# Memory value products placed inside the causal attention of a two-block transformer kernel

## The reference, cut to what matters

```python
mem_n = rms_norm(mem, mem_norm_w)
y_rnn = recurrent_group(...)
y_att = chunk_band_attention(q, k, v, rel_bias)      # 8 heads of 64, causal by chunks of 64
mixed = concatenate([rms_norm(y_rnn, gn_rnn_w), rms_norm(y_att, gn_att_w)])
x = x + mixed @ w_out
h = rms_norm(x, ln2_w)
k = mem_n @ wk                                       # memory keys
v = mem_n @ wv                                       # memory values: 256 x 1024
x = x + memory_cross_attention(h, ...)
```

## Time and profile before

| what | us |
|---|---|
| median of 3 runs | 2440.44 (2439.38 to 2442.5) |
| the profiled execution, its own time | 2438.64 |
| its span, first to last instruction | 2436.5 |
| PE, DVE, ACT, POOL busy in the span | 2192.2, 1583.9, 1187.4, 207.2 |
| memory value products on PE | 191.6 to 217.1 |
| causal attention, first shift on DVE to last values on PE | 221.3 to 286.9 |

### The profile page before, as it was taken

The page is one execution under the profiler, slowest core; times in us unless marked ns, Lnnn a source line. Parts: engine busy times, 40 slices in busy tenths (PEclk is TensorE's granted clock), DMA queues, the critical chain, the costliest instruction groups (busy, mean ns, idle before and its releaser), DMA issues.

```text
span 2436.5 us, 27159 instructions
## 1 busy us (share of the span) xinstructions
PE 2192.2 (90%) x10362; PEld 1740.6 (71%) x10362; DVE 1583.9 (65%) x1884; ACT 1187.4 (49%) x1437; POOL 207.2 (9%) x155
## 2 busy tenths in 40 slices
PE   6987798959999999994897989999989888999997
PEld 4785577648788788783764768888766566888885
DVE  6435643338888888886578576465658857655565
ACT  4534534237777777775456442222245564222223
POOL 1000000020011010110001002011100100210120
PEclk9998899979999999997899999999999999999998
DMA  5232031357999999994310022222322001222321
GB/s 196 87 139 104 1 121 52 138 157 261 359 360 353 357 363 360 351 350 183 122 52 35 25 80 103 88 91 102 110 79 87 35 1 70 104 96 90 108 87 52
DMA packets 48814, 359.98 MB, mean 148 GB/s; under 512 B 12224, under 2 KB 13416, under 8 KB 21456
## 3 DMA queue, kind: packets, MB, share of 16 engines
q1 hardware_dynamic: 36880, 340.89, 37.9%
q0 software_dynamic: 10752, 13.60, 1.8%
q10 hardware_dynamic: 1088, 4.19, 0.4%
HBM read 360.71 MB, written 25.72 MB: 159 GB/s over the span
## 4 chain that ended last, share of the span: by engine, by line
PE 75%; DVE 10%; ACT 9%; issue 3%; DMA 2%; POOL 0%; ACTq 0%; SPq 0%; DVEq 0%; POOLq 0%
PE bank L1029 39%; PE bank L496 15%; PE bank L1940 10%; DVE split_products L560 3%; ACT split_products L724 2%; PE bank L1965 2%; PE bank L1742 1%; PE bank L486 1%; PE bank L1756 1%; ACT S L1806 1%; PE bank L1727 1%; DVE split_weights L1235 1%; DVE X L1280 1%; ACT S L759 1%; DMA S<-rows_scratch,idx 1%
## 5 line engine op out<-in xcount | busy, mean ns | idle before, releaser
L1029 PE MATMUL bank<-split_x_high,split_weights 128*128 128x512 f32 x2144 | 670.9, 393 | 31.2 <-DVE split_x_low L1249 14.7
L1243 ACT ACTIVATE split_weights<-ring 128x2048 fp32r<-128x2048 f32 (+1 forms) x122 | 228.2, 1872 | 657.7 <-PE bank L1029 523.7
L1029 PEld LDWEIGHTS bank<-split_x_high,split_weights 128*128 128x128 f32 x2144 | 406.6, 190 | 121.4 <-issue 36.8
L1235 DVE TENSOR_TENSOR split_weights<-ring,split_weights 128x2048 fp32r<-128x2048 f32 (+1 forms) x122 | 276.6, 2268 | 224.7 <-ACT split_weights L1243 224.6
L1029 PE MATMUL bank<-split_products,split_weights 128*128 128x512 f32 x1200 | 333.2, 394 | 4.5 <-DVE split_products L1435 4.5
L1029 PE MATMUL bank<-split_x_low,split_weights 128*128 128x512 f32 x800 | 312.9, 391 | 0.0
L1029 PEld LDWEIGHTS bank<-split_products,split_weights 128*128 128x128 f32 x1200 | 228.6, 191 | 53.8 <-DVE split_products L1435 6.0
L496 PE MATMUL bank<-split_products 128*128 128x512 f32 x768 | 188.9, 395 | 11.9 <-DVE split_products L560 11.9
L496 PE MATMUL bank<-split_x_high,split_products 128*128 128x512 f32 x768 | 190.0, 397 | 8.0 <-DVE split_x_high L560 8.0
L496 PE MATMUL bank<-split_x_low,split_products 128*128 128x512 f32 x768 | 189.9, 397 | 6.5 <-DVE split_x_low L560 4.4
L560 DVE TENSOR_TENSOR split_products<-ring,split_products 128x2048 fp32r<-128x2048 f32 x63 | 144.4, 2293 | 57.4 <-ACT split_products L724 57.3
(11 more groups left out here) (421 smaller groups left out, 2978.5 us busy)
## 6 DMA issues: line engine op xcount, KB each, us to landing
ring<-in_expert_down_w SPq DMA_DIRECT2D x32, 2048.0 KB, 9.1
ring<-in_expert_gate_w SPq DMA_DIRECT2D x31, 2048.0 KB, 8.8
ring<-in_expert_up_w SPq DMA_DIRECT2D x31, 2048.0 KB, 8.1
ring<-in_ffn_w_up SPq DMA_DIRECT2D x44, 1024.0 KB, 4.8
ring<-in_w_in SPq DMA_DIRECT2D x26, 1024.0 KB, 4.8
ring<-in_ffn_w_down SPq DMA_DIRECT2D x16, 1024.0 KB, 4.8
ring<-in_w_out SPq DMA_DIRECT2D x12, 1024.0 KB, 4.8
ring<-in_ffn_w_down SPq DMA_DIRECT2D x8, 768.0 KB, 4.1
```

The costliest lines, as they stand in the source:

```text
L1029: mm = pe.matmul(acc[:, :], w[:, u, k, m], x, start=first and q == 0, stop=last and q == 2)
L1235: st.tell(dve.tensor_tensor(w[:, 1, 0:ks, 0:nc_], raw_half(g)[:, :, 0:nc_], as_f32(w[:, 0, 0:ks, 0:nc_]), ALU.subtract), wl_done)
L1243: st.tell(act.activation(WHL[g % 2][:, 0, 0:ks, 0:nc_], raw_half(g)[:, :, 0:nc_], ACT.Copy), wh_done)
```

## The change

The memory value products leave their place ahead of the attention and are made inside it: PE's `pe_pairs` gets a function `fill`, called in each step between the values of `p - 2` and the transposes of `p - 1`. In each odd step `memory_values(p)` makes one of the eight tiles, number `n = p // 2`, in bank 2 or 3. To leave these two banks free, the scores use banks 0 and 1 alone: a key `depth` (1 here, 2 in the second block's attention, as before) says over how many pairs the score banks turn, and scores of `p` wait for the shifts of `p - depth`. The evacuations (ACT, L2238) go into ACT's `inside` at odd `p`, `unit_high(16)` to `unit_high(19)` stand behind every second one of them (`p` = 3, 7, 11, 15), `unit_low(16)` to `unit_low(18)` in DVE's `inside` at `p` = 4, 8, 12 and `unit_low(19)` after the loop; `unit_low(14)` and `(15)` move ahead of the recurrent norm. The high and low parts of the recurrent branch leave the loop: ACT's four copies stand behind the last square and ahead of `root(2, HC)`, DVE's four subtractions behind `unit_low(19)`.

```diff
--- before.py
+++ after.py
@@ -218,7 +218,7 @@
                     scores=[(Q[r, j, tt], K[r, j, 0:keys]) for h, r, tt in halves(j, t)],
                     bias=[H[:, h, T - keys:T] for h, r, tt in halves(j, t)],
                     values=[(r, lambda kt, h=h: V[:, kt, h * 64:(h + 1) * 64]) for h, r, tt in halves(j, t)]))
-        att_cfg.append(dict(pairs=pairs, sems=att, dest=lambda c: S[:, 12 + c, :]))
+        att_cfg.append(dict(pairs=pairs, depth=1, sems=att, dest=lambda c: S[:, 12 + c, :]))
         units = []
         QX = QKVG[:, 0:8, :]
         for h in range(XHEADS):
@@ -956,7 +956,7 @@
                     values = [(r, lambda kt, h=h: VF[:, kt, 64 * (h - 4):64 * (h - 4) + 64]) for h, r, tt in halves(j, t)]
                 l_pairs.append(dict(j=place, t=t, keys=T, scores=scores, values=values, bias=None, scale=float(64 if j < 2 else HM) ** -0.5))
         att_chunk = (6, 7, 2, 3)
-        l_cfg = dict(pairs=l_pairs, sems=latt, dest=lambda c: XH[:, att_chunk[c], :], low=True)
+        l_cfg = dict(pairs=l_pairs, depth=2, sems=latt, dest=lambda c: XH[:, att_chunk[c], :], low=True)
 
         def layer_sync(sp):
             final = sp.value_load(table_u[0:1, 62:63], min_val=MINB - 1, max_val=MAXB - 1)
@@ -1712,7 +1712,7 @@
             layer_gpsimd(pool, st)
 
 
-        def pe_pairs(pe, cfg, l, first=None):
+        def pe_pairs(pe, cfg, l, first=None, fill=None):
             s, pairs = cfg["sems"], cfg["pairs"]
             before, outs = 2 * len(pairs) * l, len(pairs) // TT * l
             for step in range(len(pairs) + 2):
@@ -1722,9 +1722,9 @@
                     if first:
                         first("scores", p)
                     for i, (q, k) in enumerate(x["scores"]):
-                        if p >= 2:
-                            pe.wait_ge(s["shifted"], before + 2 * (p - 2) + i + 1)
-                        pe.matmul(bank[2 * (p % 2) + i][:, 0:x["keys"]], q, k, start=True, stop=True).then_inc(s["scored"], 1)
+                        if p >= cfg["depth"]:
+                            pe.wait_ge(s["shifted"], before + 2 * (p - cfg["depth"]) + i + 1)
+                        pe.matmul(bank[2 * (p % cfg["depth"]) + i][:, 0:x["keys"]], q, k, start=True, stop=True).then_inc(s["scored"], 1)
                 p = step - 2
                 if 0 <= p:
                     x = pairs[p]
@@ -1742,6 +1742,8 @@
                             mm = pe.matmul(bank[7 - x["j"] % 2][r, t], v(kt), PT[:, i, kt, t], start=(kt == 0), stop=(kt == last))
                             if kt == last:
                                 mm.then_inc(s["summed"], 1)
+                if fill:
+                    fill(step)
                 p = step - 1
                 if 0 <= p < len(pairs):
                     x = pairs[p]
@@ -1772,7 +1774,7 @@
                     dve.wait_ge(s["scored"], before + u + 1)
                     if p >= 2:
                         dve.wait_ge(s["turned"], before + u - 3)
-                    src = bank[2 * (p % 2) + i][:, 0:n]
+                    src = bank[2 * (p % cfg["depth"]) + i][:, 0:n]
                     if x["bias"]:
                         st.tell(dve.tensor_tensor(SS[:, u % 4, 0:n], src, x["bias"][i], ALU.add), s["shifted"])
                         st.wait()
@@ -2010,10 +2012,25 @@
             for u in range(4):
                 split_unit(10 + u, **tiles(A_XK + 2 * u), count=mem_in, n=MEM)
             rms("gn_rnn", ((a_add, 8, SUM),))
-            for u in range(4):
-                token_unit(14 + u, A_XV + 2 * u, 2, *mem_in)
+            pe.wait_ge(tile_free, A_XV)
+
+            def memory_values(p):
+
+                if p % 2 and p < 2 * DC:
+                    n = p // 2
+                    g = 14 + n // 2
+                    pe.wait_ge(wl_done, g + 1)
+                    if n >= 2:
+                        pe.wait_ge(tile_free, A_XV + n - 1)
+                    tok = slice((n % 2) * P, (n % 2 + 1) * P)
+                    hi, lo = mem_in
+                    for k in range(DC):
+                        for q, (u, x) in enumerate(((0, hi(k)), (0, lo(k)), (1, hi(k)))):
+                            mm = pe.matmul(bank[2 + n % 2][:, 0:256], x[:, tok], WHL[g % 2][:, u, k, :], start=(k == 0 and q == 0), stop=(k == DC - 1 and q == 2))
+                    mm.then_inc(tile_done, 1)
+
+            pe_pairs(pe, att_cfg[0], 0, fill=memory_values)
             pe.wait_ge(tile_free, A_XQ)
-            pe_pairs(pe, att_cfg[0], 0)
             rms("gn_att", ((a_add, 10, SUM), (a_sq, 16, square[1])))
 
             res = lambda n: dict(n0=n, done=res_done, free=res_free)
@@ -2157,27 +2174,27 @@
             dve.wait_ge(s_biasd, 32)
             for m in range(1, HC):
                 add_squares(DC, m, HC)
-            unit_low(dve, st, 12)
-            unit_low(dve, st, 13)
+            for g in range(12, 16):
+                unit_low(dve, st, g)
             dve.wait_ge(a_rstd, 2)
             for c in range(HC):
                 st.tell(dve.scalar_tensor_tensor(G[:, c, :], G[:, c, :], col("gn_rnn", c), rstd[:, :], ALU.mult, ALU.mult), a_hn)
-            for g in range(14, 20):
-                unit_low(dve, st, g)
             dve.wait_ge(s_bias, 1)
 
             def inside(p):
 
-                if 4 <= p < 8:
-                    c = p - 4
-                    dve.wait_ge(a_hi, DC + c + 1)
-                    st.tell(dve.tensor_tensor(MIXL[c], G[:, c, :], as_f32(MIX[:, c, :]), ALU.subtract), a_lo)
+                if p in (4, 8, 12):
+                    unit_low(dve, st, 15 + p // 4)
                 if p == 10:
                     add_squares(DC + HC, 1, HC)
                 if p == 14:
                     add_squares(DC + HC, 2, HC)
 
             dve_pairs(dve, st, att_cfg[0], 0, inside)
+            unit_low(dve, st, 19)
+            for c in range(HC):
+                dve.wait_ge(a_hi, DC + c + 1)
+                st.tell(dve.tensor_tensor(MIXL[c], G[:, c, :], as_f32(MIX[:, c, :]), ALU.subtract), a_lo)
             normed_split(2, DC + HC, HC, lambda c: S[:, 12 + c, :], lambda c: col("gn_att", c), lambda c: S[:, 12 + c, :],
                          lambda c: (MIXL[4 + c], as_f32(MIX[:, 4 + c, :])))
 
@@ -2233,9 +2250,9 @@
 
             n = [0]
 
-            def evac(dst, src, func=ACT.Copy, scale=1.0):
+            def evac(dst, src, func=ACT.Copy, scale=1.0, b=None):
                 act.wait_ge(tile_done, n[0] + 1)
-                st.tell(act.activation(dst, src(bank[n[0] % 4]), func, scale=scale), tile_free)
+                st.tell(act.activation(dst, src(bank[n[0] % 4 if b is None else b]), func, scale=scale), tile_free)
                 n[0] += 1
 
             full = lambda b: b[:, :]
@@ -2310,15 +2327,14 @@
                 for c in range(2 * u, 2 * u + 2):
                     evac(KM[:, c, :], half)
             root(1, HC)
-            for u in range(4):
-                unit_high(act, st, 16 + u)
-                for t in range(2):
-                    evac(VM[:, t, u * 256:(u + 1) * 256], half)
 
             def inside(p):
 
-                if 3 <= p < 7:
-                    high(DC + p - 2, MIX[:, p - 3, :], G[:, p - 3, :])
+                if p % 2:
+                    m = p // 2
+                    evac(VM[:, m % 2, (m // 2) * 256:(m // 2 + 1) * 256], half, b=2 + m % 2)
+                    if m % 2:
+                        unit_high(act, st, 16 + m // 2)
                 if p in (5, 9, 13):
                     c = (p - 5) // 4
                     act.wait_ge(att["att_out"], c + 1)
@@ -2330,6 +2346,8 @@
             act.wait_ge(a_add, 9)
             st.wait()
             st.tell(act.activation(square[1], S[:, 15, :], ACT.Square), a_sq)
+            for c in range(HC):
+                high(DC + c + 1, MIX[:, c, :], G[:, c, :])
             root(2, HC)
             for c in range(HC):
                 high(DC + HC + c + 1, MIX[:, 4 + c, :], S[:, 12 + c, :])
```

## The result

| what | us |
|---|---|
| the changed kernel, median of 4 runs | 2417.01 (2415.89 to 2420.97) |
| the kernel before, median of 4 runs beside it | 2439.91 (2438.31 to 2442.5) |
| ratio | 0.9907, 95% interval 0.9894 to 0.9921 |
| span of the profiled execution | 2415.2 (before 2436.5) |

What follows compares the result with a forecast made beforehand. PE was taken as the overall bound, with DVE fullest in the attention and the value products on the chain ahead of it. -32.0 + 8.8 + 1.8 = -21.4 us took the median 2440.44 to 2419.0, range 2411 to 2430.

Steps and rivals of the forecast that it cites:

- Term 1: Ahead of the attention: DVE's first shift moves from 221.30 to about 189.3, -32.0 us.
- Term 2: From DVE's first shift to its last scaling: the inserted work lengthens the loop from 60.3 to 69.1 us, +8.8.
- Two score banks: Attention scores on PE: turning over two banks costs 0, as PE waits longer anyway; 7.5 us if the cover were gone.
- Term 3: Behind the last scaling: four recurrent copies ahead of the root delay chunk 4 of `w_out`, +1.8 us.
- The clock: PE's granted clock over the attention loop: over 0.9 instead of 0.78; about 3 us more if it fell as before.
- All kept behind it: Rest of the first block and expert loads: this chain starts everything there, so the whole -21.4 us is kept.
- in series: Rival, attention loop: every tile delays DVE by its whole 2.9 us, loop +26.3, total -4 (2436.5); 6%.
- All hidden: Rival, attention loop: PE's tiles fit everywhere, only ACT's high part shows, loop +3.1, total -27 (2413); 8%.
- Half hidden: Rival, attention loop: low clock at several tiles, or the banks, cost 3 to 10 us more, total -18 to -11; 13%.
- Slower: Rival, attention loop: PE stays at half clock, each tile adds 5.3 us, loop +45.5, total +15 (2456); 3%.

Runs made afterwards that it cites:

- the first experiment: The kernel before with only the causal scores put in two banks and nothing moved; 2441.57 us against 2441.12, ratio 1.0001.
- the early tile: The changed kernel with the first memory value tile made in step 0 instead of step 1; 2416.07 us and, again, 2416.30, against 2416.44.
- the tiles of 3: The changed kernel with 3 matmuls a tile instead of 24; 2413.89 us, ratio 0.9888 to the kernel before.

## Why the prediction was right

It was right in sign, size and mechanism: -21.4 forecast, -22.9 between the medians, -21.3 between the spans. That the spans meet it to 0.1 is partly luck: the loop cost 0.7 more than forecast, the tail 1.1 less, the norm began 0.6 earlier, and 1.2 were lost behind `ln3`. By its own steps:

- **Term 1, the start, -32.0.** Measured 34.69 - 2.65 = 32.0 behind the norm. The edit does two things here, and no run separates them: it moves the products into the loop, and it makes the low parts 14 and 15 ahead of the norm. In the kernel before PE stood still for one of these:

```profile
191.61 25.45 PE L1965 MATMUL bank<-split_weights,split_mixed 128*128 128x256 f32 x192 [10.66 <-DVE split_weights L1235]
```

  The high part of unit 14 was ready at 176.3, so the low parts moved alone would have let the products begin up to 10.7 us earlier, where they stood. Without that pause they might also have run at the full clock from the start (192 at the 0.119 of the earlier trace rows are 22.9, 2.5 less). By this estimate 10 to 13 of the 32 us, and so of the 21, could be had without interleaving; it was not tried.
- **Term 2, the loop, +8.8.** Measured 69.86 - 60.35 = +9.5. Of its parts: the waits for the exponential 1.48 three times (1.7 said), before tile 0 0.57, 0.56 and none (0.8, 0.8, 0.2), before tile 2 0.75 three times (0.7). The one that was mis-sized is the first tile: 3.49 us of wait where 1.9 was said. I let PE's clock rise within that tile (4.2 us); in this trace the whole tile ran at the half clock, 5.35, close to the 5.3 that the earlier trace rows give. Where a trace has a first tile of 4.10 us, the wait is 2.24. The other waits came out 1.2 smaller in sum, so the term as a whole was off by 0.7 only.
- **Two score banks, 0.** Shown by the first experiment, ratio 1.0001, for a loop without tiles. The waits for shifts exist there (7.5 us on PE's weight loads) and stand where PE would wait for ACT's copies anyway. The Trainium skill's advice to turn over several banks (Perfetto Trace Analysis, Optimizing Tensor Performance, Matmuls), by which the sum would have been about -13, is not borne out there. In the changed kernel one such wait is not free: the scores of pair 1 wait 6.43 us for the first shift (the PE row at 189.02), and the first tile stands behind them. So the first tile's 3.49 is in part the price of the two banks; the early tile, put ahead of these scores, takes it away.
- **Term 3, the tail, +1.8.** Measured +1.0 to the root (7.74 against 6.73), and +0.7 to chunk 4 of `w_out`, which is how the term was counted (13.90 against 13.2, 0.4 of slack used up). The 2.2 us of copies are there; what was left out is that the last transposes and the values ahead of them now run at clock 1.00 (0.88 and 1.10 us instead of 1.55 and 1.97), of which 1.1 reaches the root. The two runs without tiles of full size show the other end: clock 0.50 in the same 7 us and a tail of 9.7.
- **The clock.** Said above 0.9, measured 0.95 in the loop. The tiles hold the clock up in the loop and beyond it, and a loop thinned to 3 matmuls a tile falls to 0.85 and then 0.50. With that the traces agree in both directions with the Trainium skill (TensorE: Matmul & The Clock Gate, Why this matters for your kernels), which has gaps in PE's work bring back the half clock.
- **All kept behind it.** Up to the root of `ln3` the trace is 22.4 us ahead (451.2 against 473.6), 21.2 ahead of the expert loop (499.5 against 520.7), 21.0 behind it (1140.7 against 1161.7), 21.3 at the end. The 1.2 us went between `ln3` and the expert loop, in products that no edit touched. First the kernel before, then the changed one:

```profile
515.71 2.98 PE L496 MATMUL bank<-split_x_low,split_products 128*128 128x512 f32 x12 [2.10 <-DVE split_products L646]
```

```profile
493.01 4.44 PE L496 MATMUL bank<-split_x_low,split_products 128*128 128x512 f32 x12 [2.10 <-DVE split_products L646]
```

  The granted clock around them was 1.00 before and 0.75 after. The changed kernel run again has 4.44 there too, three variants have 4.2 to 4.4, and the other kernels 3.0. What decides it is not shown.

Of the rivals, "in series" is excluded by the tiles of 3: 7.3 us of 22.2 show, not all. "All hidden" is excluded by the waits for scores. "Half hidden" wanted 3 to 10 us more in the loop, and 0.7 came. "Slower" wanted the half clock at every tile; it was seen in the first alone.

## What to carry to other kernels

Work that needs neither the result nor the time of a loop's fullest engine belongs in the gaps of the others, but it has a price that can be summed ahead: walk the fullest engine's program and ask, at each of its waits, what the inserted piece puts ahead of the instruction that it waits for. Here 25 us of matmuls cost 7 us and their weight preparation 7 more of work and 4 of waits, where 8 us of other waits and work went away. The pieces around the matmuls (where the high and low parts stand, in which step the first tile runs) were worth a further 5.7 us in the loop, without touching the matmuls. A double buffer may be given up where its engine is held by a later wait anyway; try that alone first, it is one edit, and look again once the insert stands behind it. And before a piece is moved, see what it waits for where it stands: here 10.7 us of its lateness was one operation put too late in another engine's program.

## What was not expected of the hardware

- Filling PE's gaps changed its speed outside them: with nearly the same PE instructions behind the last scaling, the granted clock was 1.00 with tiles of 24 in the loop, 0.74 in the kernel before, and 0.50 with tiles of 3 or none and no split in the loop. That moved the tail by up to 2 us (7.7 against 9.7), as much as the edits under study.
- The expert loop, the same code at the same mean clock of 0.96, took from 639.3 to 644.6 us in the traces. In one of two traces that hid an edit that had taken 2.6 us out of the attention.
- The same 12 products behind `ln3` took 3.0 us in some traces and 4.4 in others, by the clock granted there, so that 1.2 us of a difference in time can come from a place far from the edit.
